# Hybrid RWKV-7 and windowed-attention block, one core: the scan's operands in the order of reading, early query loads, a bank per head's scores, low-rank products from unscaled x

## What is computed

```python
h = rms_norm(x, ln1_g)
p = h @ w_in                       # 2560 columns: r k v | wd ad gd | q ka va
p_rwkv = p + (prev - p) * mu_prev + (next - p) * mu_next      # centred token shift
decay, a, g = low_rank(wd), low_rank(ad), low_rank(gd)        # from 256 columns of p
# group A: 8 heads x 64, in both directions of time:
S = S * w + (S @ a) b^T + v k^T;   y = S @ r
# group B: 8 query heads, 2 kv heads, |t-s| <= 128, 128-query blocks
s = q k^T / 8 - slope * |t - s|;   o = softmax([s, sink])[:-1] @ v
x = x + concat(o_rwkv, o_att) @ w_out
x = x + (gelu(conv3(h2 @ w_gate)) * (h2 @ w_up)) @ w_down     # h2 = rms_norm(x, ln2_g)
return rms_norm(x, lnf_g)
```

## Time and profile before

| | |
|---|---|
| median of 3 runs | 1778.2 us (1778.07 to 1786.06) |
| profiled execution | 1778.3 us, its span 1776.2 us |
| mean granted TensorE clock | 0.911 |
| busy: PE, DVE, ACT, POOL | 87%, 45%, 26%, 3% of the span |
| DMA | 148.40 MB, 186999 packets, mean 84 GB/s |

### The profile page before, as it was taken

One profiled execution on the slowest core, in us unless ns is written; L12 is line 12 of the kernel. 1 busy time (PEld: TensorE's weight loads), 2 busy tenths in 40 slices (PEclk: granted clock), 3 DMA queues, 4 the chain that ended last, 5 costly groups with the idle time before them and its releaser, 6 DMA issues.

```text
span 1776.2 us, 27480 instructions
## 1 busy us (share of the span) xinstructions
PE 1537.7 (87%) x11156; PEld 1140.4 (64%) x11156; DVE 796.0 (45%) x975; ACT 467.2 (26%) x686; POOL 45.9 (3%) x45
## 2 busy tenths in 40 slices
PE   0797888979569899888579699999999999999994
PEld 0344445454257677777458478888788888788883
DVE  4244736569235565666553543332223332233335
ACT  2131332310013344434412232331012220022221
POOL 0000000011000000000100000000000000000000
PEclk9999999989857888767689799999999999999997
DMA  4007165273654555553111011111111111111112
GB/s 162 27 24 194 65 139 156 61 195 97 153 159 100 145 138 143 148 128 101 59 36 47 35 36 47 47 47 48 47 48 47 47 47 48 55 39 53 41 36 95
DMA packets 186999, 148.40 MB, mean 84 GB/s; under 512 B 100464, under 2 KB 166128, under 8 KB 184784
## 3 DMA queue, kind: packets, MB, share of 16 engines
q1 hardware_dynamic: 182672, 136.48, 27.4%
q0 software_dynamic: 1728, 5.64, 1.1%
q10 hardware_dynamic: 2560, 5.77, 1.0%
HBM read 106.04 MB, written 41.81 MB: 83 GB/s over the span
## 4 chain that ended last, share of the span: by engine, by line
PE 77%; DVE 9%; SPq 6%; issue 3%; ACT 3%; DMA 2%; DVEq 0%; ACTq 0%
PE banks L477 45%; PE banks L465 14%; PE banks L672 2%; PE banks L630 2%; PE banks L590 2%; PE banks L640 2%; PE banks L600 2%; PE banks L681 2%; PE banks L544 2%; PE banks L657 1%; PE banks L484 1%; SPq L324 1%; DVE hT L1050 1%; PE banks L611 1%; SPq L347 1%
## 5 line engine op out<-in xcount | busy, mean ns | idle before, releaser
L465 PE MATMUL banks<-hT,work 128*128 128x512 f32 x640 | 283.6, 603 | 29.3 <-issue 17.5
L477 PE MATMUL banks<-h_hi,w_hi 128*128 128x512 f32 x832 | 259.5, 393 | 27.3 <-DVE h_lo L1031 14.2
L477 PE MATMUL banks<-h_lo,w_hi 128*128 128x512 f32 x832 | 257.9, 391 | 0.0
L477 PE MATMUL banks<-h_hi,w_lo 128*128 128x512 f32 x832 | 257.8, 391 | 0.0
L465 PEld LDWEIGHTS banks<-hT,work 128*128 128x128 f32 x640 | 122.8, 193 | 187.8 <-issue 178.5
L477 PEld LDWEIGHTS banks<-h_hi,w_hi 128*128 128x128 f32 x832 | 156.8, 189 | 65.2 <-issue 28.2
L922 ACT ACTIVATE w_hi<-work 128x1024 fp32r<-128x1024 f32 x76 | 80.2, 1057 | 383.2 <-PE banks L477 383.2
L477 PEld LDWEIGHTS banks<-h_lo,w_hi 128*128 128x128 f32 x832 | 157.6, 189 | 33.1
L477 PEld LDWEIGHTS banks<-h_hi,w_lo 128*128 128x128 f32 x832 | 157.2, 189 | 32.9
L1298 DVE TENSOR_TENSOR xT<-xT,banks 128x1024 f32<-128x1024 f32 (+1 forms) x32 | 39.1, 1221 | 240.0 <-PE banks L477 240.0
L477 PE MATMUL banks<-g_hi,w_hi 128*128 128x512 f32 x352 | 108.4, 389 | 0.0
(11 more groups left out here) (156 smaller groups left out, 1749.1 us busy)
## 6 DMA issues: line engine op xcount, KB each, us to landing
work<-in_w_gu SPq DMA_DIRECT2D x44, 512.0 KB, 3.6
work<-in_w_in SPq DMA_DIRECT2D x20, 512.0 KB, 3.2
AR_d<-work SPq DMA_DIRECT2D x8, 1024.0 KB, 6.1
G_d<-work SPq DMA_DIRECT2D x8, 1024.0 KB, 4.8
BK_d<-work SPq DMA_DIRECT2D x32, 256.0 KB, 5.7
work<-AR_d SPq DMA_DIRECT2D x32, 256.0 KB, 3.4
work<-G_d SPq DMA_DIRECT2D x32, 256.0 KB, 3.8
work<-BK_d SPq DMA_DIRECT2D x32, 256.0 KB, 3.9
```

What stands on the lines that cost most here:

```text
L465: mm = pe.matmul(out[:, h * HALF:(h + 1) * HALF], wt[:, k, :], src[:, k, h * HALF:(h + 1) * HALF], start=(k == 0), stop=(k == kn - 1))
L477: mm = pe.matmul(out[:, h * HALF:(h + 1) * HALF], wp[slot][:, k, :], xp[:, k, h * HALF:(h + 1) * HALF], start=(k == 0 and p_ == 0), stop=( ...
```

## The change

Five edits:

1. AR, G and BK lie in one DRAM tensor `scan_d` (direction, chunk pair, partition, table, pair, 128 numbers), so that one DMA with a row of 6 KB per partition loads a chunk pair of one direction; the stores write pieces of 512 bytes (AR, G) and 256 bytes (BK). The gram matrices are read back in four DMAs where there were two. TI_d and y_d are laid out in the order of reading as well: rows of 1 KB instead of pieces of 256 bytes.
2. `load_qk` of the next iteration is issued ahead of `store_y` of step 2.
3. The scores of head h go to bank 4 + h instead of 4 + h % 2; PE no longer waits for `sc_out` between them, but for `o_out` before the fourth, whose bank the values share.
4. The two low-rank products are made from xg = x * gain, without the reciprocal root, tile by tile as x arrives; VectorE multiplies their result by `rs`. The norm matmul stands between them and writes another bank pair.
5. The start's loads are reordered: par, then x with the first tile of w_in, the tables behind.

```diff
-        AR_d = dram("AR_d", (2, NPAIR, P, NC * 2 * C))
-        G_d = dram("G_d", (2, NPAIR, P, NC * 2 * C))
-        BK_d = dram("BK_d", (2, NPAIR, P, NC * HD))
-        TI_d = dram("TI_d", (2, NPAIR, 2, C, NC * C))
+        scan_d = dram("scan_d", (2, NC // 2, P, 3, NPAIR, P))
+        TI_d = dram("TI_d", (2, 2, C, NC, NPAIR, C))
...
+            sp.dma_start(par[:, :], a["par"]).then_inc(s["par_loaded"], 16)
+            sp.dma_start(xT[:, 0, :], a["xT"][:, 0, :]).then_inc(x_loaded[0], 16)
+            sp.dma_start(W3[0], a["w_in"][0]).then_inc(w_full[0], 16)
+            for k in range(2, KD, 2):
+                sp.dma_start(xT[:, k, :], a["xT"][:, k, :]).then_inc(x_loaded[k // 2], 16)
...
-                    src = G_d[z][bass.ds(j, 1), 64 * e:64 * e + C].rearrange("o s (c x) -> (o c) s x", x=2 * C)[:, :, 0:C]
-                    sp.dma_start(M[z][C * j:C * (j + 1), e, :, :], src).then_inc(M_loaded[z], 16)
+                    for q in range(2):
+                        sp.dma_start(M[z][C * j + q:C * (j + 1):2, e, :, :],
+                                     scan_d[z, :, 64 * e:64 * e + C, 1, j, 2 * C * q:2 * C * q + C])\
+                          .then_inc(M_loaded[z], 16)
...
-                    sp.dma_start(AR_d[z][pair].rearrange("o p n -> (o p) n"), AR.rearrange("p c a t -> p (c a t)"))\
-                      .then_inc(s["AR_stored"], 16)
+                    sp.dma_start(scan_d[z, :, :, 0, j, :].rearrange("c p n -> p c n"),
+                                 AR.rearrange("p (c q) a t -> p c (q a t)", q=2)).then_inc(s["AR_stored"], 16)
...
-                    for dst, src, n in ((ARs, AR_d, 2 * C), (Gs, G_d, 2 * C), (BKs, BK_d, HD)) if given else ():
-                        sp.dma_start(dst[slot][:, z], src[z].rearrange("j p n -> p j n")[:, :, bass.ds(c * n, 2 * n)])\
+                    if given:
+                        sp.dma_start(AGB[slot][:, z].rearrange("p m j n -> p (m j n)"),
+                                     scan_d[z, bass.ds(both, 1)].rearrange("o p m j n -> (o p) (m j n)"))\
...
                     for slot in range(2):
-                        store_y(i, 2 * slot)
                         if slot == 1:
                             sp.wait_ge(s["sc_out"], 8 * i + 8)
                             load_qk(i + 1)
+                        store_y(i, 2 * slot)
                         store_y(i, 2 * slot + 1)
...
-                    if h < 2:
-                        if behind:
-                            pe.wait_ge(s["pt_out"], 3 * blk - 3 + FREE)
-                    else:
-                        pe.wait_ge(s["sc_out"], 4 * blk + h - 1)
-                    pe.matmul(banks[:, 4 + h % 2, 0:BAND], qs[64 * e:64 * e + 64, 2 * g + hh, :],
+                    if behind and h == heads[0]:
+                        pe.wait_ge(s["pt_out"], 3 * blk - 3 + FREE)
+                    if behind and h == GH - 1:
+                        pe.wait_ge(s["o_out"], blk - 1 + FREE)
+                    pe.matmul(banks[:, 4 + h, 0:BAND], qs[64 * e:64 * e + 64, 2 * g + hh, :],
...
+            for k in range(KD):
+                dve.wait_ge(x_loaded[k // 2], 32)
+                ts(xg[:, k, :], xT[:, k, :], col("ln1", k), None, ALU.mult).then_inc(s["xg_ready"], 1)
+                if k:
+                    add_square(0, k)
...
+            scale_by_rms(0)
+            for k in range(KD):
+                stt(hT[:, k, :], xT[:, k, :], col("ln1", k), rs, ALU.mult, ALU.mult).then_inc(ns["scaled"], 1)
+            shift_low_rank(0, lora)
+            scale_by_rms(1)
+            shift_low_rank(1, sgT[:, :])
```

## The result

The changed kernel takes 1699.8 us (median of four runs, 1696.2 to 1701.9) beside 1778.5 for the kernel before on the same chip: a ratio of 0.9554, 95% interval 0.953 to 0.9577. The forecast was 1689, in a range of 1658 to 1733. The profiled execution took 1701.9 us, with a span of 1700.1 against 1776.2.

What follows compares the result with a forecast made beforehand. TensorE, busy 87% of the span, was taken as the bound, with time to win only where it idles or runs at its lower clock. Start, pair loop, before the scan, scan: 1778.3 - 37 + 10 - 3.5 - 59 = 1689 us, range 1658 to 1733.

Steps and rivals of the forecast that it cites:

- The start: Up to the end of the pair loop's first product: 100.3 to 63.3 us, 37 us saved, between 32 and 40.
- Root 1.1: In the start, after the norm matmul: the root takes 1.1 us, then the reciprocal 6.55, ending at 36.7.
- The pair loop: 512-byte AR and G stores delay the low-rank weights 3.5 us in each of three turns: 10 us lost, bounds 0 and 30.
- my own sign of being wrong: Stated sign of a wrong forecast: pair loop turns longer by much more than 3.5 us.
- what PE waits for is paid twice: In the scan: as the wait and as slower matmuls after it, 32 taking 1.97 us at 1.2 GHz, 1.15 at 2.4.
- Before the scan: The first two operand sets load in 6 KB rows, 8.0 us in place of 11.5: 3.5 us won, between 0 and 5.
- The lower bound that I had named: Before the scan: 0 us won, if another landing, va_d's, holds the queue.
- The scan: Separate score banks and early table loads bring 355.5 us to 296: 59 us won, between 20 and 80.
- rival 1: In the scan, PE waits for S or U in place of logits; gain only 20 us: 1728 us, chance 0.22.
- rival 2: In the scan, operand loads come late, 2 us 14 times; gain only 35 us: 1713 us, chance 0.07.
- rival 3: Pair loop stores, pieces far apart in DRAM, run far below 155 GB/s: slower, 1787 us or more, chance 0.02.
- rival 4: 512-byte pieces move as fast as long rows: no 10 us lost, no 3.5 won, 1682 us, chance 0.05.

Runs made afterwards that it cites:

- Experiment 12: The kernel before with AR and G alone stored as 512-byte pieces, gram loads in 4 DMAs: 1800.2 us, ratio 1.0126.
- experiment 9: The kernel before with each gram load asked for in 4 DMAs in place of 2, all else as before: 1782.3 us, ratio 1.0032.
- experiment 1: The kernel before with the new start alone (x first in the queues, low-rank products from unscaled x): 1747.1 us, ratio 0.9818.
- Experiment 4: The changed kernel with the next pair's low-rank weights asked for ahead of the AR and G stores: 1669.5 us, ratio 0.9385.
- experiment 7: The changed kernel with low-rank weights early in the queue and the inverses' stores and loads ahead of the wait for va_d: 1670.0 us, ratio 0.9384.
- experiment 8: The changed kernel with low-rank weights and inverses both moved earlier in the queue, but the old DRAM layout: 1670.2 us, ratio 0.9387.
- experiment 5: The kernel before with the score banks and the early query loads, old layout and old start: 1708.9 us, ratio 0.963.
- experiment 2: The kernel before with the new DRAM layout alone, 10 loads for a set in place of 14: 1798.6 us, ratio 1.0118.
- experiment 6: The changed kernel with the second direction's inverse stores and both directions' inverse loads ahead of the wait for va_d: 1693.5 us, ratio 0.9532.

## Why the forecast came out as it did

The profiled execution is 13 us above the forecast. The misses are 2.5, 14.6 and 4.0 us to the slow side in the first three stages and 7.7 us to the fast side in the scan. So part of how near the total came is luck: what the pair loop lost beyond its price was half made up by a scan priced too low.

**The start** (37 forecast, 34.5 measured). Two steps failed. "PE follows tile by tile and has finished product 0 by 27": PE began only at 11.63, when its weights were there, and ran the product for 16.32 us, so the norm's matmul ended at 29.7 in place of 28.8. VectorE's sums, on which I rested this moment, were done 3.4 us before they were of use. And "Root 1.1": the table load in front of it had been hidden and is no longer, 1.3 us. The rest of the chain, reciprocal, multiplication, scalings and product, took the forecast durations within 0.3 us.

**The pair loop** (10 forecast, 24.6 measured). This is the term that was mis-sized, and my own sign of being wrong came true: the turns, measured from the first gram products of one to those of the next, are longer by 7.7 to 9.6 us and not by 3.5. Its mechanism held: three stores of 1 MB at some 290 GB/s, weights some 4 us later, and PE's waits 11.2 us longer in sum. Experiment 12 shows the stores as the cause, and experiment 9 leaves the number of DMAs only 0.65 us of the lateness. That 3.5 us for three stores came out so exactly is in part luck: I had them at 273 GB/s, and they moved at 290. What the sum left out I had written myself in the first paragraph, that "what PE waits for is paid twice". I applied it to the scan and not to these waits. The clock's fall costs another 10.6 us at the twelve matmuls behind the waits, 21.8 with the waits themselves. The remaining 2.8 us are a balance of smaller things. The first 128 matmuls of a turn's gram products take 5.50 us in three turns where the kernel before has 3.95, against which ScalarE's waits of 0.75 to 0.88 us behind the weights go away. In the first turn the 5.50 stand ahead of any late weights, and experiments 1 and 4 have them there as well, so they are not the weights' doing. Experiment 4 takes the weights out of the stores' way and brings back 24.7 us.

**Before the scan** (3.5 forecast, 0.5 lost). The lower bound that I had named came true: va_d's landing holds the queue for 9.2 us. What I did not see is that the layout itself brings this wait, since va_d lands 13.4 us after it is asked for in place of 7.4. As a size the 3.5 us of the long rows were near: experiments 7 and 8, where the inverses are loaded ahead of this wait, differ by 3.3 us.

**The scan** (59 forecast, 66.7 measured). Iteration 0 took 40.2 for 40, iterations 1 to 4 together 129 for 130, the last three 119.7 for 126. Iteration 0 is no safe hit, since two kernels with the same banks took 35 us for it. The last three were mis-sized: I let 6.5 of VectorE's extra 7.4 us come up as idle time of PE, on top of iterations of 32.5; it was 2.5 to 5.2 us, and steady iterations are 31.5. The mean clock of the whole scan, 0.89, is just under the 0.9 that I had named, but it stayed at 0.83 to 0.88 there, where the earlier trace rows had 0.67. That the loads are hidden held, and more than I had said: experiment 5 shows the same steady iteration with the old loads. The early query loads were worth far more than the 3.7 us at which I had priced their wait. With the banks alone that wait grew to 10.8, and the whole kernel was 23 us slower than with both (1732.2 and 1708.9).

**The rivals.** The wait moved only in small part (rival 1): PE's waits at the state and U lines, which it names, are 6.7 us in all, 4.1 the largest, where 27.7 us of waits at the score line went away. No load was late (rival 2). The layout did not sink the kernel (rival 3), but alone it is a loss of 1.2%. Pieces of 512 bytes do not move as fast as long rows (rival 4). The rule that the Trainium skill gives on the page "DMA: Bandwidth & Descriptors", under Specifications, line rate from 512 bytes, would have left the pair loop alone; experiment 12 has 291 GB/s at a full DMA share where the earlier trace rows has 390.

Still open is why iterations differ between runs of nearly the same code, the late ones by 3 us (38.1 or 41.1 us for iteration 6), the first by 5 and more. No experiment was made for that.

## What to carry to other kernels

A late landing in front of TensorE costs its wait and then, after every wait of 4.2 us or more here, another 3.6 us in slower matmuls; price both wherever an edit makes a full queue longer. A layout that helps the reader makes the writer's pieces shorter, and it pays only where the reader waits: here the reads inside the scan were hidden and the writes stood ahead of small weights that needed only an earlier place in the queue. And when a gate goes away, look at every transfer that it had been holding back, since the one that nobody waits for may be the first to start.

## What the runs showed that I had not expected

The length of one wait does not tell whether the clock falls behind it. In the kernel before, a wait of 2.37 us was followed by matmuls at full clock. In experiment 9 three turns went like this:

```profile
176.21 3.81 PE L485 MATMUL banks<-work 64*128 64x512 f32 x12 [2.24 <-DMA work<-in_lora_w]
...
250.21 6.74 PE L485 MATMUL banks<-work 64*128 64x512 f32 x12 [1.79 <-DMA work<-in_lora_w]
...
327.85 5.48 PE L485 MATMUL banks<-work 64*128 64x512 f32 x12 [1.18 <-DMA work<-in_lora_w]
```

The longest wait left the level alone and the shortest did not. So waits that grew by only 1.8 us in sum (5.2 against 3.4) went with 7 us in the pair loop (372.4 against 365.4), and moving small edits in or out of such a stretch can cost or give more than the wait itself shows. After every wait of 4.21 us or more for these weights, twelve waits in four kernels (the changed one and experiments 2, 6 and 12), the matmuls behind ran at the lower level throughout (7.36 us).

The time that SyncE's queue spends on a DMA's issue depends on its neighbours. The same store of AR held the queue for 1.95 us in the kernel before and for 0.64 in experiment 9, where the loads next to it held it longer. The DMA engines were full in both, and there only the length of the whole stretch can be compared.
